# Column sums of the modulation by transposition and a VectorE reduction; head and norm spreads by transposition

## The chip, the core and the metric

The kernel runs on one core of a Trainium2 chip. The metric is the device time of one execution in microseconds (us), the median of several runs. The profile shows one execution; its times are counted from the start of its span.

## The reference, cut to what matters

Two layers work on x of 1024 tokens by 1024 features, all in f32: layer 0 mixes tokens by sliding-window attention, layer 1 by gated spatial mixing, and each is followed by a dense MLP. Each of the four sub-layers starts with a norm that is modulated by a vector made from c:

```python
cond = jax.nn.silu(c)
for i in range(DEPTH):                                   # DEPTH = 2
    mod = (cond @ mod_w[i] + mod_b[i])[:, None, :]       # mod_w[i]: 1024 x 6144
    shift1, scale1, gate1, shift2, scale2, gate2 = jnp.split(mod, 6, axis=-1)
    h = rms_norm(x, norm1_gain[i]) * (1 + scale1) + shift1
    y = swa_sink_attention(...) if i == 0 else gmlp_spatial_gating(...)
    x = x + gate1 * y
    h = rms_norm(x, norm2_gain[i]) * (1 + scale2) + shift2
    x = x + gate2 * squared_relu_mlp(h, w1[i], w2[i])
```

`rms_norm` divides each token by the root of its mean square over the features. In the attention, the queries of each head (64 features) are normed in the same way, and rotated by their position.

## The kernel before, in words

Features lie on the 128 partitions, tokens along the free dimension; x is 8 tiles of 128 x 1024. Every large product is made of units: 128 output features by 1024 tokens, 8 steps over the input features, each step three products (high by high, high by low, low by high, in a reduced f32 type that TensorE streams in one pass) for each half of 512 tokens. These are the matmuls of L1095, 48 a unit, 194 units. Units alternate between the PSUM tensors `pp[0]` and `pp[1]`. ScalarE makes the high part of a weight block (`split_hi`, L305) when the unit that used the buffer two units ago is done, GpSimd the low part (`split_lo`, L274), TensorE waits for it in `ready`. The engines run separate programs, and only semaphores tie them. The order of work on TensorE is written out by hand: small work is put between the steps of a unit by hooks.

**Modulation.** Its 12 parts (shift, scale, gate, twice a layer) of 1024 values each are sums over the 1024 features of c. VectorE multiplies rows of `mod_w` by a value of silu(c) for each partition and adds them up in `mod_acc` (128 x 1024; L668, L815). What is left is the sum over partitions. `mod_columns` (L1160 to L1167) does it on TensorE: eight f32 products with 128 columns of `mod_acc` as the weights and one column of ones as the moving operand write eight columns of `pp[3]`. VectorE's `mod_part` (L678 to L685, or L822 for parts 0 and 1) adds the bias, writes `mod`, and clears `mod_acc`. Parts 0 and 1 are made ahead of the first product, from `mod_acc` and from `tmp`, into different columns of `pp[3]`; part 2 is made in the stage of the queries, part 3 ahead of the attention, 4 and 5 in its output projection (5 inside `closing_pair`), 6 to 9 in the first MLP, 10 and 11 in the gated mixing.

**Head norms.** For five units (four of queries, one of keys), TensorE sums squares (`token_sums`, L1172), ScalarE takes the root, VectorE the reciprocal, and ScalarE copies each value 32 wide into `tmp` (L391). TensorE's `spread` (L1179) turns that by eight f32 products of 128 x 128 with the identity, so that features lie on partitions again; VectorE then rotates (L864 to L879).

**Norms 1 to 3** run half by half over `closing_pair` and `opening_pair`: TensorE sums squares (`token_squares`, L1187), ScalarE takes the root (L320), VectorE's `deviations` (L687 to L694) takes the reciprocal and writes the four values of a half as four diagonal matrices of 128 x 128 into `mod_t` (L691), and TensorE's `spread_norm` (L1195) multiplies them by a matrix of ones, which puts each token's value on all partitions. VectorE waits for it (`bc_done`), then scales x (L748) and makes the low part of h (L756), ScalarE makes the high part between the two (L341); TensorE's opening steps wait for that (`h_done`). Norm 0 has the same steps on whole rows.

`pp[3]` also takes the transposed values (L1236, which ScalarE copies at L447) and half of the attention's scores (L1246), and `pp[2]` the transpositions of the gated mixing (`v_turn`, L1344).

Of the kernel before, what the change touches and what calls it, by code (L numbers as in the profile page):

```python
# [14 lines left out]
P = 128  # L15
KC = D // P
HALF = 512
# [31 lines left out]
def build(nc, x_in, c_in, pos_in, weights, mod_w, cols, mats, ws_in, bias_in, q_dram, v_dram, out):  # L49
    f32, f32r, i32 = mybir.dt.float32, mybir.dt.float32r, mybir.dt.int32  # L50
    ALU = mybir.AluOpType
# [3 lines left out]
    with ctx:  # L55
        def sb(name, shape, dt=f32, where=ctx):
            return where.enter_context(nc.sbuf_tensor(name, shape, dt))

        def sem(name):
            return ctx.enter_context(nc.semaphore(name))  # L60
# [13 lines left out]
        vscale = sb("vscale", [P, 2, KC])  # L74
        root = sb("root", [P, 4 * KC])
        inv = sb("inv", [P, 4 * KC])
        qgain = sb("qgain", [P, 2])


# [94 lines left out]
        ws_ld, wsz = sem("ws_ld"), sem("wsz")  # L174
        sp_mm, t_mul, t_hi = sem("sp_mm"), sem("t_mul"), sem("t_hi")
        late_in = [sem("late_in0"), sem("late_in1")]
        acc_zero = sem("acc_zero")
        saved = sem("saved")


# [16 lines left out]
        def columns_of(half):  # L197
            return slice(HALF * half, HALF * half + HALF)
# [451 lines left out]
        def _(dve):  # L650
# [27 lines left out]
            def mod_part(part):  # L678

                dve.wait_ge(mod_mm, part + 1)  # L680
                V.tensor_tensor(out=mod[:, bass.ds(part, 1), :].rearrange("p a k -> p (a k)"),
                                in0=pp[3][:, HALF:HALF + KC], in1=colt[:, bass.ds(part * KC + 4 * KC, KC)],
                                op=ALU.add).then_inc(mod_done, 1)
                V.memset(mod_acc[:, :], 0.0).then_inc(acc_zero, 1)
                dve.wait_ge(acc_zero, part)  # L685

            def deviations(n, half):  # L687

                dve.wait_ge(sd_done, 2 * n + half + 1)
                own(V.reciprocal(inv[:, 4 * half:4 * half + 4], root[:, 4 * half:4 * half + 4]))  # L690
                V.tensor_tensor(out=mod_t[:, 0, columns_of(half)].rearrange("p (b m) -> p b m", m=P),  # L691
                                in0=ident[:, :].unsqueeze(1).to_broadcast([P, 4, P]),
                                in1=inv[:, 4 * half:4 * half + 4].unsqueeze(2).to_broadcast([P, 4, P]),
                                op=ALU.mult).then_inc(rb_done, 1)  # L694

            def gains(n):
                dve.wait_ge(mod_done, 3 * n + 2)
# [121 lines left out]
                        deviations(0, half)  # L819
            for part in range(2):  # L820
                dve.wait_ge(mod_mm, part + 1)
                V.tensor_tensor(out=mod[:, part, :], in0=pp[3][:, HALF * (1 - part):HALF * (1 - part) + KC],  # L822
                                in1=mod_b(part), op=ALU.add).then_inc(mod_done, 1)
            norm(0)
            V.memset(mod_acc[:, :], 0.0).then_inc(acc_zero, 1)
            dve.wait_ge(acc_zero, 1)
# [254 lines left out]
        def _(pe):  # L1081
# [75 lines left out]
                            spread_norm(n, 1)  # L1157
                last.then_inc(gemm, 1)

            def mod_columns(part, counter, count, acc=None, place=HALF):  # L1160

                pe.wait_ge(counter, count)
                acc = mod_acc[:, :] if acc is None else acc
                for k in range(KC):
                    last = T.matmul(pp[3][:, place + k:place + k + 1], acc[:, P * k:P * k + P], ones[:, 0:1],
                                    start=True, stop=True)
                last.then_inc(mod_mm, 1)  # L1167

            def token_sums(heads, select, counter):
# [6 lines left out]
            def spread(counter):  # L1176

                for b in range(KC):
                    last = T.matmul(pp[2][:, P * b:P * b + P], tmp[:, 1, P * b:P * b + P], ident[:, :],  # L1179
                                    start=True, stop=True)  # L1180
                last.then_inc(counter, 1)

            def token_squares(n, half):
# [8 lines left out]
            def spread_norm(n, half):  # L1192

                pe.wait_ge(rb_done, 2 * n + half + 1)
                T.matmul(pp[2][:, columns_of(half)], ones[:, :], mod_t[:, 0, columns_of(half)],  # L1195
                         start=True, stop=True).then_inc(bc_done, 1)

            pe.wait_ge(const_in, 48)
            for half in range(2):
# [1 line left out]
            mod_columns(0, mf_used, KC)  # L1201
            for half in range(2):
                spread_norm(0, half)
            mod_columns(1, mf_used, 2 * KC, tmp[:, 0, :], 0)

            def head_squares(j):

# [23 lines left out]
            for j in range(4):  # L1231
                if j:
                    pe.wait_ge(v_cp, j)
                for r in range(4):
                    n = 4 * j + r
                    last = T.transpose(pp[3][:, P * r:P * r + P], vt[:, CHUNK * n:CHUNK * n + P], ident[:, :])  # L1236
                last.then_inc(v_tr, 1)
            mod_columns(3, mt_used, 2 * KC)


# [78 lines left out]
            def mlp(layer):  # L1319
                pair0 = U_MLP[layer] // 2  # L1320
                opening_pair(pair0, 2 * layer + 1)
                h_units(pair0, 1)

                def down(g, close=None):
                    columns = (lambda: mod_columns(g + 6, mt_used, g * KC + (RING_MLP + KC))) if layer == 0 else None
                    hid_units(g * 8 + (pair0 + 4), g * KC + HID_MLP[layer], columns, close)

                down(0)
                with pe.Fori(1, MLP_GROUPS - 1 + layer) as g:
                    h_units(g * 8 + pair0, 0)  # L1330
                    down(g)
                if layer == 0:
                    h_units((MLP_GROUPS - 1) * 8 + pair0, 0)
                    down(MLP_GROUPS - 1, 2)
# [127 lines left out]
```

## Time and profile before

| | |
|---|---|
| median of 3 runs | 2522.09 us (2521.42 to 2524.6) |
| profiled execution | 2525.77 us, of which span 2523.8 us |
| TensorE busy | 96% of the span, mean granted clock 0.979 of full speed |
| VectorE, ScalarE, GpSimd busy | 40%, 25%, 20% |
| DMA | 189 MB, 75 GB/s mean |

A row of the timeline shows the start, then the length from the first start to the last end of a run of equal instructions, the engine, the line, the names out<-in, the shape and how many, and in brackets how long the engine had been idle and what ended that. The length of a matmul holds its way through the array; what a matmul costs in a stream is the distance from its start to the next one's. An f32 product appears as two records.

### The profile page before, as it was taken

The numbers are of one execution on the slowest core, as the hardware profiler recorded it, in microseconds if no ns is written. First come the engines' busy times: TensorE is split into PE (matmuls) and PEld (weight loads), VectorE is DVE, ScalarE is ACT, GpSimd is POOL, SyncE is SP. The second block draws the span as 40 slices with busy tenths as digits, with TensorE's granted clock in tenths as the row PEclk, the third lists the DMA queues.
The fourth block names the chain that finished last, engine by engine and source line by source line (L and its number), as shares of the span: only waits on it lengthen the run. The fifth ranks groups of instructions, "written<-read, shape, count | busy, mean of one in ns | idle before, by whom it ended". The sixth has DMA issues, their size and how long they took to land.

```text
span 2523.8 us, 28427 instructions
## 1 busy us (share of the span) xinstructions
PE 2418.9 (96%) x10592; PEld 1937.7 (77%) x10592; DVE 1011.1 (40%) x1088; ACT 633.1 (25%) x768; POOL 506.3 (20%) x232
## 2 busy tenths in 40 slices
PE   3997999999999999998999999999899999999999
PEld 2776677788888888886788888888688888888887
DVE  7664756532432333334432541343623322223232
ACT  3322622321221212222322221121321221222221
POOL 1111321121212212121211112112122212222121
PEclk9996999999999999998999999999899999999999
DMA  6342141221311211211333321221111111111112
GB/s 245 101 140 74 48 163 42 75 70 47 100 59 58 84 66 57 93 55 37 124 127 125 108 82 50 66 68 50 34 42 50 42 50 50 42 50 49 43 50 83
DMA packets 70594, 189.05 MB, mean 75 GB/s; under 512 B 23440, under 2 KB 25360, under 8 KB 70032
## 3 DMA queue, kind: packets, MB, share of 16 engines
q1 hardware_dynamic: 52144, 127.64, 15.8%
q10 hardware_dynamic: 18400, 60.69, 6.8%
q8 instruction: 37, 0.61, 0.1%
q14 instruction: 13, 0.11, 0.0%
HBM read 170.48 MB, written 16.78 MB: 74 GB/s over the span
## 4 chain that ended last, share of the span: by engine, by line
issue 64%; PE 28%; POOL 8%; POOLq 0%; DVE 0%; ACT 0%; DVEq 0%
PE pp L1095 28%; POOL w_lo L274 7%; POOL pr L286 1%; POOLq L294 0%; POOLq L273 0%; DVE x L969 0%; DVE mod_t L665 0%; ACT tmp L314 0%; POOLq L285 0%; POOLq L290 0%; POOLq L280 0%; POOL kf L277 0%; POOLq L274 0%; DVEq L969 0%; POOL vt L278 0%
## 5 line engine op out<-in xcount | busy, mean ns | idle before, releaser
L274 POOL TENSOR_TENSOR w_lo<-w_raw,w_hi 128x1024 fp32r<-128x1024 f32 x194 | 472.5, 2436 | 1922.9 <-ACT w_hi L305 1922.8
L1095 PE MATMUL pp<-h_hi,w_hi 128*128 128x512 f32 x1824 | 603.3, 406 | 35.2 <-DVE h_lo L756 23.3
L1095 PE MATMUL pp<-h_lo,w_hi 128*128 128x512 f32 x1824 | 592.8, 401 | 0.0
L1095 PE MATMUL pp<-h_hi,w_lo 128*128 128x512 f32 x1824 | 592.1, 400 | 0.0
L1095 PEld LDWEIGHTS pp<-h_hi,w_hi 128*128 128x128 f32 x1824 | 345.3, 192 | 127.8 <-issue 21.2
L305 ACT ACTIVATE w_hi<-w_raw 128x1024 fp32r<-128x1024 f32 x194 | 205.0, 1057 | 910.1 <-PE pp L1095 831.4
L1095 PEld LDWEIGHTS pp<-h_lo,w_hi 128*128 128x128 f32 x1824 | 348.9, 191 | 84.9 <-issue 1.0
L1095 PEld LDWEIGHTS pp<-h_hi,w_lo 128*128 128x128 f32 x1824 | 348.1, 191 | 85.1
L1095 PE MATMUL pp<-hid_hi,w_hi 128*128 128x512 f32 x1280 | 410.3, 398 | 0.0
L1095 PE MATMUL pp<-hid_lo,w_hi 128*128 128x512 f32 x1280 | 408.8, 396 | 0.0
L1095 PE MATMUL pp<-hid_hi,w_lo 128*128 128x512 f32 x1280 | 408.8, 396 | 0.0
L969 DVE SCALAR_TENSOR_TENSOR x<-pp,mod,x 128x1024 f32 (+1 forms) x82 | 104.8, 1278 | 493.8 <-PE pp L1095 493.7
L1095 PEld LDWEIGHTS pp<-hid_lo,w_hi 128*128 128x128 f32 x1280 | 241.1, 188 | 59.1 <-issue 0.5
L1095 PEld LDWEIGHTS pp<-hid_hi,w_lo 128*128 128x128 f32 x1280 | 241.1, 188 | 58.8
L1095 PEld LDWEIGHTS pp<-hid_hi,w_hi 128*128 128x128 f32 x1280 | 240.6, 188 | 58.5 <-issue 0.5
L993 DVE SCALAR_TENSOR_TENSOR tmp<-pp,tmp 128x1024 f32<-128x1024 f32 x64 | 78.4, 1224 | 335.9 <-ACT tmp L544 335.9
L665 DVE TENSOR_TENSOR mod_t<-mod_t,tmp 128x1024 f32<-128x1024 f32 x82 | 153.6, 1873 | 95.8 <-ACT tmp L314 95.0
L544 ACT ACTIVATE tmp<-pp 128x1024 f32<-128x1024 f32 x64 | 65.7, 1027 | 472.2 <-PE pp L1095 472.2
L996 DVE TENSOR_TENSOR hid_lo<-tmp,hid_hi 128x1024 f32 x64 | 119.3, 1864 | 87.0 <-ACT hid_hi L547 87.0
L668 DVE SCALAR_TENSOR_TENSOR mod_acc<-mod_t,cond,mod_acc 128x1024 f32<-128x1024 f32 x64 | 95.6, 1494 | 55.6 <-DMA mod_t<-mod_w 54.3
L314 ACT ACTIVATE tmp<-x 128x1024 f32 (+1 forms) x82 | 86.9, 1061 | 81.7 <-DVE x L969 73.6
L547 ACT ACTIVATE hid_hi<-tmp 128x1024 f32 x64 | 67.9, 1062 | 35.4 <-DVE tmp L993 35.4
(132 smaller groups left out, 1134.3 us busy)
## 6 DMA issues: line engine op xcount, KB each, us to landing
w_raw<-weights SPq DMA_DIRECT2D x194, 512.0 KB, 3.3
mod_t<-mod_w ACTq DMA_DIRECT2D x64, 512.0 KB, 3.4
mod_first<-mod_w SPq DMA_DIRECT2D x16, 512.0 KB, 15.5
mod_late<-mod_w ACTq DMA_DIRECT2D x2, 4096.0 KB, 19.1
v_dram<-v_out ACTq DMA_DIRECT2D x16, 512.0 KB, 5.3
vf<-v_dram ACTq DMA_DIRECT2D x16, 512.0 KB, 3.3
x<-x_in SPq DMA_DIRECT2D x4, 1024.0 KB, 9.0
qf<-q_dram SPq DMA_DIRECT2D x32, 128.0 KB, 2.5
```

What stands on the lines that cost most here:

```text
L274: nc.gpsimd.tensor_tensor(out=w_lo[:, s, :, :], in0=w_raw[:, s, :, :], in1=w_hi[:, s, :, :].bitcast(f32), op=ALU.subtract).then_inc(lo_don ...
L286: nc.gpsimd.tensor_tensor(out=pr[:, b, :, 0:P], in0=pr[:, b, :, 0:P], in1=small[:, b, 3, :].unsqueeze(2).to_broadcast([P, 4, P]), op=ALU.m ...
L305: nc.scalar.activation(w_hi[:, s, :, :], w_raw[:, s, :, :], ACT.Copy).then_inc(hi_done, 1)
L314: nc.scalar.activation(tmp[:, s, :], x[:, bass.ds(k, 1), :].rearrange("p a s -> p (a s)"), ACT.Square).then_inc(sq_done, 1)
L544: nc.scalar.activation(tmp[:, s, :], pp[s][:, :], ACT.Relu).then_inc(relu, 1)
L547: nc.scalar.activation(hid_hi[:, bass.ds(i * 2 + s, 1), :].rearrange("p a s -> p (a s)"), tmp[:, s, :], ACT.Copy).then_inc(hd_hi, 1)
L665: V.tensor_tensor(out=sumsq, in0=sumsq, in1=tmp[:, s, :], op=ALU.add).then_inc(ss_done, 1)
L668: V.scalar_tensor_tensor(out=mod_acc[:, :], in0=tile, scalar=cond[:, 2, bass.ds(k, 1)], in1=mod_acc[:, :], op0=ALU.mult, op1=ALU.add).then ...
L969: V.scalar_tensor_tensor(out=xn, in0=pp[s][:, :], scalar=mod[:, gate, bass.ds(i * 2 + s, 1)], in1=xn, op0=ALU.mult, op1=ALU.add).then_inc( ...
L993: V.scalar_tensor_tensor(out=tmp[:, s, :], in0=pp[s][:, :], scalar=0.0, in1=tmp[:, s, :], op0=ALU.max, op1=ALU.mult).then_inc(evac[s], 1)
L996: V.tensor_tensor(out=hid_lo[:, bass.ds(i * 2 + s, 1), :].rearrange("p a s -> p (a s)"), in0=tmp[:, s, :], in1=hid_hi[:, bass.ds(i * 2 + s ...
L1095: last = T.matmul(pp[s][:, cs], w[:, s, k, :], r[:, k, cs], start=(k == 0 and w is w_hi and r is hi), stop=(k == KC - 1 and w is w_lo))
```

## The change

`mod_columns` turns the eight blocks of `mod_acc` by transpositions into all 1024 columns of `pp[3]`, and VectorE sums each block of 128 columns by a reduction into `col_sum`, waits for it, and adds the bias. As all columns are written, TensorE waits for the part before (`mod_done`), and ahead of part 3 for the last copy of the values (`v_cp`). `spread` and `spread_norm` become transpositions with the identity; `deviations` writes each value 128 wide by a copy where it wrote diagonals.

```diff
             def mod_part(part):
                 dve.wait_ge(mod_mm, part + 1)
+                V.tensor_reduce(out=col_sum[:, :], in_=pp[3][:, :].rearrange("p (k c) -> p k c", c=P), axis=X,
+                                op=ALU.add).then_inc(col_summed, 1)
+                dve.wait_ge(col_summed, part + 1)
                 V.tensor_tensor(out=mod[:, bass.ds(part, 1), :].rearrange("p a k -> p (a k)"),
-                                in0=pp[3][:, HALF:HALF + KC], in1=colt[:, bass.ds(part * KC + 4 * KC, KC)],
+                                in0=col_sum[:, :], in1=colt[:, bass.ds(part * KC + 4 * KC, KC)],
                                 op=ALU.add).then_inc(mod_done, 1)
...
-                V.tensor_tensor(out=mod_t[:, 0, columns_of(half)].rearrange("p (b m) -> p b m", m=P),
-                                in0=ident[:, :].unsqueeze(1).to_broadcast([P, 4, P]),
-                                in1=inv[:, 4 * half:4 * half + 4].unsqueeze(2).to_broadcast([P, 4, P]),
-                                op=ALU.mult).then_inc(rb_done, 1)
+                V.tensor_copy(mod_t[:, 0, columns_of(half)].rearrange("p (b m) -> p b m", m=P),
+                              inv[:, 4 * half:4 * half + 4].unsqueeze(2).to_broadcast([P, 4, P])).then_inc(rb_done, 1)
...
             for part in range(2):
                 dve.wait_ge(mod_mm, part + 1)
-                V.tensor_tensor(out=mod[:, part, :], in0=pp[3][:, HALF * (1 - part):HALF * (1 - part) + KC],
-                                in1=mod_b(part), op=ALU.add).then_inc(mod_done, 1)
+                V.tensor_reduce(out=col_sum[:, :], in_=pp[3][:, :].rearrange("p (k c) -> p k c", c=P), axis=X,
+                                op=ALU.add).then_inc(col_summed, 1)
+                dve.wait_ge(col_summed, part + 1)
+                V.tensor_tensor(out=mod[:, part, :], in0=col_sum[:, :], in1=mod_b(part), op=ALU.add).then_inc(mod_done, 1)
...
-            def mod_columns(part, counter, count, acc=None, place=HALF):
+            def mod_columns(part, counter, count, acc=None):
                 pe.wait_ge(counter, count)
+                if part is not None:
+                    pe.wait_ge(mod_done, part)
                 acc = mod_acc[:, :] if acc is None else acc
                 for k in range(KC):
-                    last = T.matmul(pp[3][:, place + k:place + k + 1], acc[:, P * k:P * k + P], ones[:, 0:1],
-                                    start=True, stop=True)
+                    last = T.transpose(pp[3][:, P * k:P * k + P], acc[:, P * k:P * k + P], ident[:, :])
                 last.then_inc(mod_mm, 1)
...
             def spread(counter):
                 for b in range(KC):
-                    last = T.matmul(pp[2][:, P * b:P * b + P], tmp[:, 1, P * b:P * b + P], ident[:, :],
-                                    start=True, stop=True)
+                    last = T.transpose(pp[2][:, P * b:P * b + P], tmp[:, 1, P * b:P * b + P], ident[:, :])
...
             def spread_norm(n, half):
                 pe.wait_ge(rb_done, 2 * n + half + 1)
-                T.matmul(pp[2][:, columns_of(half)], ones[:, :], mod_t[:, 0, columns_of(half)],
-                         start=True, stop=True).then_inc(bc_done, 1)
+                for b in range(4 * half, 4 * half + 4):
+                    last = T.transpose(pp[2][:, P * b:P * b + P], mod_t[:, 0, P * b:P * b + P], ident[:, :])
+                last.then_inc(bc_done, 1)
...
-            mod_columns(1, mf_used, 2 * KC, tmp[:, 0, :], 0)
+            mod_columns(1, mf_used, 2 * KC, tmp[:, 0, :])
...
+            pe.wait_ge(v_cp, 4)
             mod_columns(3, mt_used, 2 * KC)
```

The calls for parts 6 to 9 pass `None`, and so don't wait for `mod_done`.

## Rows read from the trace of the kernel before

**Rows 1.** The page: busy time by engine.
```profile
PE 2418.9 (96%) x10592; PEld 1937.7 (77%) x10592; DVE 1011.1 (40%) x1088; ACT 633.1 (25%) x768; POOL 506.3 (20%) x232
```
**Rows 2.** Who waited for whom on TensorE from 230 us on (us, times, longest).
```profile
PE pp L1095 <- DVE h_lo L756: 23.3, 12, 4.0
```
**Rows 3.** Timeline of TensorE around the columns of part 6.
```profile
549.07 1.84 PE L1165 MATMUL pp<-ones,mod_acc 128*128 128x1 f32 x16
550.77 0.71 PE L1095 MATMUL pp<-hid_hi,w_hi 128*128 128x512 f32 x2
```
**Rows 4.** Timeline of TensorE around a `v_turn` (a transposition of eight blocks).
```profile
1228.02 1.03 PE L1344 MATMUL pp<-ident,tmp 128*128 128x128 f32 x8
1228.81 0.71 PE L1095 MATMUL pp<-h_hi,w_hi 128*128 128x512 f32 x2
```
**Rows 5.** Timeline of the query stage, TensorE, then VectorE.
```profile
133.13 1.95 PE L1179 MATMUL pp<-ident,tmp 128*128 128x128 f32 x16
134.83 0.71 PE L1095 MATMUL pp<-h_hi,w_hi 128*128 128x512 f32 x2
...
157.57 1.84 PE L1172 MATMUL pp<-colt,tmp 128*128 128x4 f32 x16
...
135.11 1.22 DVE L864 TENSOR_TENSOR tmp<-cos,pp 128x1024 f32<-128x1024 f32 x1 [7.35 <-PE pp L1179]
...
154.90 1.22 DVE L859 TENSOR_TENSOR tmp<-tmp 128x1024 f32<-128x1024 f32 x1
```
**Rows 6.** Lines of VectorE, shapes apart (count, then busy us, mean ns).
```profile
L911 DVE TENSOR_REDUCE small<-pp 128x4 f32<-128x516 f32 x30 | 20.5, 685 | 1.3 <-PE pp L1246 1.3
```
**Rows 7.** VectorE operations with one SBUF source (L1041: duration ns min, median, max).
```profile
74.80 0.69 DVE L830 TENSOR_SCALAR cos<-sin 128x1024 f32<-128x1024 f32 x1
...
L1041 DVE TENSOR_SCALAR vf<-vf,vscale x128: 330/336/2501, 1405.5 to 1682.4; 128x128 f32<-128x128 f32 x128
```
**Rows 8.** Timeline ahead of the attention.
```profile
227.68 3.41 PE L1165 MATMUL pp<-ones,mod_acc 128*128 128x1 f32 x16
234.18 3.78 PE L1246 MATMUL pp<-kf,qf 64*128 64x128 f32 x16 [3.09 <-DMA kf<-oa]
```
**Rows 9.** Timeline of the gated mixing after part 11.
```profile
1399.32 0.17 DVE L681 TENSOR_TENSOR mod<-pp,colt 128x8 f32<-128x8 f32 x1 [4.10 <-PE pp L1165]
...
1407.03 0.61 ACTq L617 DMA_DIRECT2D bias<-bias_in  x1
...
1410.29 2.02 PE L1370 MATMUL pp<-ws,vf 128*128 128x128 f32 x16 [1.05 <-issue]
```
**Rows 10.** Timeline of the closing and opening of norm 1.
```profile
423.91 1.02 PE L1195 MATMUL pp<-mod_t,ones 128*128 128x512 f32 x2
...
425.00 0.39 PE L1095 MATMUL pp<-h_lo,w_hi 128*128 128x512 f32 x1
...
424.73 1.05 ACT L305 ACTIVATE w_hi<-w_raw 128x1024 fp32r<-128x1024 f32 x1
...
442.28 0.69 DVE L691 TENSOR_TENSOR mod_t<-ident,inv 128x512 f32<-128x512 f32 x1
...
449.87 1.41 DVE L748 SCALAR_TENSOR_TENSOR tmp<-x,amp,pp 128x512 f32<-128x512 f32 x2 [2.46 <-PE pp L1195]
```
**Rows 11.** Timeline of the start: GpSimd, VectorE, TensorE.
```profile
29.16 6.06 POOL L274 TENSOR_TENSOR w_lo<-w_raw,w_hi 128x1024 fp32r<-128x1024 f32 x2 [28.13 <-ACT w_hi L305]
...
33.14 2.63 DVE L691 TENSOR_TENSOR mod_t<-ident,inv 128x512 f32<-128x512 f32 x1
...
47.30 0.16 DVE L822 TENSOR_TENSOR mod<-pp,colt 128x8 f32<-128x8 f32 x1
51.05 0.17 DVE L822 TENSOR_TENSOR mod<-pp,colt 128x8 f32<-128x8 f32 x1 [3.59 <-PE pp L1165]
```
**Rows 12.** Stretches: us, busy of PE, PEld, DVE, ACT, POOL, then the granted clock.
```profile
90.00:100.00 10.00, 8.35 (x28) 7.28 (x29) 2.78 (x3) 6.25 (x7) 0.00 (x0) 0.51 0.29 95
...
1200.00:1400.00 200.00, 198.50 (x928) 160.69 (x928) 68.70 (x161) 54.94 (x56) 39.25 (x16) 1.00 0.40 131
```

More of the change, by code:

```diff
@@ L76, in build @@
         inv = sb("inv", [P, 4 * KC])
+        col_sum = sb("col_sum", [P, KC])
         qgain = sb("qgain", [P, 2])
@@ L176, in build @@
         late_in = [sem("late_in0"), sem("late_in1")]
-        acc_zero = sem("acc_zero")
+        acc_zero, col_summed = sem("acc_zero"), sem("col_summed")
         saved = sem("saved")
@@ L1324, in down @@
                 def down(g, close=None):
-                    columns = (lambda: mod_columns(g + 6, mt_used, g * KC + (RING_MLP + KC))) if layer == 0 else None
+                    columns = (lambda: mod_columns(None, mt_used, g * KC + (RING_MLP + KC))) if layer == 0 else None
                     hid_units(g * 8 + (pair0 + 4), g * KC + HID_MLP[layer], columns, close)
```

## The prediction

> **What bounds the kernel now.** I read the busy times first: TensorE is busy for 96% of the span, the others for 40% or less [rows 1]. So in most places a microsecond taken from TensorE's stream is a microsecond of the kernel, and work on VectorE is free if it fits between its waits. The waits of TensorE then show where this is not so: from the attention on, most of what it waits for is VectorE's low part of h (L756), 23.3 us in 12 waits, four in each of the three openings [rows 2]. There the chain of VectorE and ScalarE sets the time. The timeline gives three more such places: the query stage, where the rotation on VectorE and the next head norm follow each other in a ring; the start, where parts 0 and 1 must be there before the first product; and the join in the gated mixing after part 11. I cost the change at each place by what is late there.
>
> **A transposition against a product.** The columns of part 6 take 549.07 to 550.77, 1.70 us for 16 records [rows 3]. `spread` takes the same 1.70 (133.13 to 134.83) [rows 5]. A `v_turn`, which is the very call that the change uses, with eight blocks and the identity, takes 1228.02 to 1228.81, 0.79 us for 8 records, and is followed by the same first product of a unit [rows 4]. So each of both saves 1.70 - 0.79 = 0.91 us of TensorE at the full clock. `spread_norm` takes 423.91 to 425.00, 1.09 us with one product in between that costs 0.24 at the pace of its neighbours, so 0.85 [rows 10]; four transpositions are half of a `v_turn`, about 0.40 with what the first product after them loses. It saves 0.45; for VectorE's start I count 0.43.
>
> **The reduction.** It reads 1024 f32 of PSUM in one pass. The reduction of 516 takes 0.685 [rows 6], a multiply over 1024 of PSUM 1.22 [rows 5]; I take 1.22, and 0.04 for its semaphore, an estimate from gaps of VectorE's dependent pairs: 1.26 us a part. Between ends of 1.2 and 1.4 nothing changes sign. The Trainium skill, "VectorE: DVE Perf Modes", section "Rules for kernel authors", speaks against it: a reduction on the hot path is to be expected at one element a cycle, the slowest kind of VectorE work. The row agrees on the rate; whether it is on the hot path is the question of each place.
>
> **The copy in `deviations`.** The product with the identity takes 0.69 for 512 elements [rows 10]. An operation with one SBUF source does 1024 in 0.69 [rows 7], so 512 cost about 0.43: 0.26 saved. The source repeats one value 128 times, which no row shows for VectorE; the bounds are a saving of 0 and of 0.26, and I take 0.26, as the row is the nearest in kind. The Trainium skill (same page, "Mode 2×_2P") has that rate for copies in SBUF when the outermost dimension is even, which it is here (4); with its figures the result is the same.
>
> **Parts 4 to 10** lie in TensorE's stream with no idle time ahead of the next step. VectorE's 1.26 us more is covered: VectorE's evacuation after part 6 is needed only when the next unit on the other buffer is done, and a unit takes over 10 us (at most 12.5, 2418.9 us on 194 units [rows 1]). After part 4, VectorE is behind by about 1.3 us at one evacuation, but the buffer is wanted some 10 us later. The new wait for `mod_done` looks back one part and is met long before. 7 x 0.91 = 6.4 us saved. Without the cover each would cost 1.26 - 0.91 = 0.35 instead.
>
> **Part 11** is different: its L681 at 1399.32 is followed on VectorE by `mod_acc`'s clearing, the aggregates of the layer norm and a memset, which release ScalarE's last load at 1407.03, and TensorE stands idle 1.05 us until the first blend at 1410.29 [rows 9]. The chain starts 0.91 earlier and is 1.26 longer: 0.35 us lost.
>
> **The query stage: five spreads and part 2.** VectorE waits 7.35 us for the spread, then begins the rotation that leads to the next head norm [rows 5]. Both TensorE's stream and that ring start 0.91 earlier, whichever is late. Five times 0.91 is 4.55. Part 2 takes 0.91 out of the stream ahead of the next sums at 157.57. These need VectorE's sum of squares, 154.90 + 1.22 = 156.1: 1.4 us of slack. The reduction uses 0.35 of it and the earlier stream 0.91, which leaves 0.1 or more. 0.91 saved, with 0.9 at risk. Stage: 5.5 us.
>
> **Part 3** has a clock of one half: 16 records in 3.41, so eight transpositions take about 1.8 and 0.25 to the end. It now waits for ScalarE's last copy of the values, of 512 columns, for which I take 0.9 us (VectorE needs 0.69 for 516 [rows 6], and the call has to be released). 227.7 + 0.9 + 2.05 + 1.26 gives 231.9, and the bias, the clearing and the sinks, 1.6 us at most, end near 233.5. The scores wait for a DMA until 234.18 anyway [rows 8]. Cost nothing; 0.6 us of cover, queued behind it is only the clearing of a buffer. If it fails, some tenths.
>
> **The three closings and openings.** In the first half, `spread_norm` is earlier for VectorE, but ScalarE splits the next weights until 425.78 and the high part follows only then; then GpSimd's pass holds VectorE [rows 10]. That chain starts from the unit before, so I count nothing (between 0 and 0.43 each). In the second half VectorE is waited for: its copy at 442.28 releases TensorE's restart, 0.26, and it then waits 2.46 us for the second `spread_norm` until 449.87, 0.43. 3 x 0.69 = 2.1 us saved.
>
> **The start.** VectorE's first diagonals at 33.14 take 2.63 since GpSimd's pass runs until 35.22 [rows 11]; an operation with one source is held in the same way, up to 2.5 where the median is 0.34 [rows 7]. So the copies save 0.26 and 0.26, together 0.5, not 2. Against it stands a new chain: parts 0 and 1 now share the columns of `pp[3]`. TensorE must wait for part 0's reduction, and VectorE comes to that only after the sums of part 1, at 47.30 [rows 11]. Before, these ended, then the products (3.6), then 51.05. Now: 46.8 + 1.26 + 0.2 to `mod_done`, 8 transpositions at half clock 2.05, reduction 1.26: the bias is added at about 51.6. 0.6 us lost. If the copy is not held by GpSimd, the start gains 1.4 instead.
>
> **The sum.** -6.4 + 0.35 - 5.5 - 2.1 + 0.6 = -13.0 us. The profiled execution goes from 2525.77 to 2512.8, its span from 2523.8 to 2510.8; the median of the runs was 3.7 below it, so 2522.1 - 13.0 = 2509.1 us.
>
> **The rivals.**
> (a) More is gained: the first copy is not held, part 11 hides, and the first `spread_norm` counts. 2.0 + 1.26 + 1.3: 2504.5. Against it are the held rows and 1.05 us of idle time at the join. 0.10.
> (b) The reduction is on the path at every part, as at 11. Parts 2 and 4 to 10 then cost 0.35 each instead of saving 0.91: 8 x 1.26 = 10.1, and 2519.2, within 0.2%. Against it: VectorE is busy 40% [rows 1] and idle ahead of most evacuations. 0.08.
> (c) The transposition of these operands takes two records a block as the product did. No TensorE time is saved and the reductions remain: +1.3 at part 2 or 11, about +2 at the start: 2525. Against it: `v_turn` has one record a block [rows 4]. 0.02.
> (d) Slower: transpositions leave TensorE at its lower clock for a while. In the stretch from 90 to 100 us, after a stall, the granted clock is 0.51, the 1.2 GHz level, and half the time is lost [rows 12]. 13 bursts of transpositions are new in the full-speed stream outside the openings (parts 2 and 4 to 11, four spreads or more). If each cost a third of what that stretch lost, 1.6 us, it would be 21, and 2509.1 + 21 = 2530; it decides from 1.0 us each (13.0 / 13). Against it: the stretch from 1200 to 1400 has 16 `v_turn`s and a clock of 1.00 [rows 12]. 0.04. The Trainium skill, "TensorE: Matmul & The Clock Gate", section "Part 4: PE-mode transpose", says that the full clock does not engage for transpositions; the same rows speak against that for short bursts between products, and by it alone the time would be that of this rival.
> My forecast has the remaining 0.76.
>
> **How the numbers follow.** A measurement of this kernel can tell about 0.2%, 5 us, from no change. Faster by more than that are the forecast and (a): 0.86. Within it (b) and (c): 0.10. Slower: (d), 0.04. For the range I take (a) as the low end, 2504.5; upward the copy without its saving (1.3), part 2 lost (0.9), the evacuations after parts 4 and 5 late (1.8), and a restart in an opening whose clock rises later (1.5 in all): 2514.6. I widen that to 2515.5 for the scatter of medians (3 us between the runs of before).
>
> **What would show it.** Part 6 with 8 records in 0.79 us; spreads of 0.79; L911-like reductions of 1.22 on VectorE; deviations' copy of 0.43, the first one held until 35.2; part 1's transpositions starting about 48.3 and the first product at 56.2 instead of 55.67; the first blend of the gated mixing with more idle ahead of it, about 2.3 us; the granted clock unchanged. I am wrong if the copy is slow, if the ring of the query stage turns out to be timed by a DMA that does not start earlier, or if idle time appears behind the columns of parts 4 to 10.

## The result and the profile after

The changed kernel takes 2504.82 us, the median of four runs (2504.02 to 2508.65), against 2523.35 (2521.42 to 2524.68) for four runs of the kernel before beside them. The ratio is 0.993, 95% interval 0.9918 to 0.9941. The profiled execution went from 2525.77 us to 2504.02, its span from 2523.8 to 2502.1. The forecast was 2509.1 and faster; the time lies inside the range, near its low end. About 18 us were gained where 13.0 had been summed.

The lines of after stand in the order of the groups that they answer to. The page, busy time by engine (answers to [rows 1]):
```profile
PE 2386.4 (95%) x10472; PEld 1911.2 (76%) x10472; DVE 1028.7 (41%) x1100; ACT 632.5 (25%) x768; POOL 505.8 (20%) x232
```
The waits of TensorE from 230 us on (answers to [rows 2]):
```profile
PE pp L1099 <- DVE h_lo L758: 23.5, 16, 4.0
```
The timeline of TensorE, in order of time: the start [rows 11], the query stage [rows 5], ahead of the attention [rows 8], the opening of norm 1 [rows 10], the columns of part 6 [rows 3], the blend [rows 9]:
```profile
48.30 1.94 PE L1171 MATMUL pp<-ident,tmp 128*128 128x128 f32 x8 [10.81 <-DVE mod L827]
...
56.16 1.19 PE L1099 MATMUL pp<-h_hi,w_hi 128*128 128x512 f32 x2 [5.92 <-DVE h_lo L717]
...
154.82 2.62 PE L1177 MATMUL pp<-colt,tmp 128*128 128x4 f32 x16 [2.29 <-DVE tmp L863]
...
164.04 1.03 PE L1184 MATMUL pp<-ident,tmp 128*128 128x128 f32 x8
164.83 0.48 PE L1099 MATMUL pp<-h_hi,w_hi 128*128 128x512 f32 x1
...
230.24 3.78 PE L1252 MATMUL pp<-kf,qf 64*128 64x128 f32 x16 [3.64 <-DMA kf<-oa]
...
434.41 0.79 PE L1099 MATMUL pp<-h_hi,w_hi 128*128 128x512 f32 x1 [1.69 <-DVE h_lo L758]
...
539.02 1.04 PE L1171 MATMUL pp<-ident,mod_acc 128*128 128x128 f32 x8
539.81 0.72 PE L1099 MATMUL pp<-hid_hi,w_hi 128*128 128x512 f32 x2
...
1392.70 2.02 PE L1376 MATMUL pp<-ws,vf 128*128 128x128 f32 x16 [2.53 <-issue]
```
VectorE's new operations: the reductions of parts 2 to 11 by shape (count, then busy us, mean ns, then the idle time before them), and the copies of the norm roots (duration ns min/median/max) with what they replace in [rows 10, 11]:
```profile
L682 DVE TENSOR_REDUCE col_sum<-pp 128x8 f32<-128x1024 f32 x10 | 12.2, 1221 | 33.0 <-PE pp L1171 33.0
...
L695 DVE COPY mod_t<-inv x8: 426/427/2373, 33.1 to 1776.0; 128x512 f32<-128x512 f32 x8
```
And one stretch of the gated mixing (columns as in [rows 12]):
```profile
1199.01:1392.70 193.69, 191.17 (x894) 155.96 (x895) 70.20 (x174) 49.99 (x51) 38.51 (x17) 1.00 0.40 133
```
Before, the same restart of norm 1's opening:
```profile
443.69 0.79 PE L1095 MATMUL pp<-h_hi,w_hi 128*128 128x512 f32 x1 [1.96 <-DVE h_lo L756]
```
The prices hold. Part 6 takes 8 records and 0.79 us (539.02 to 539.81), a spread 0.79 (164.04 to 164.83), a reduction 1.22, a copy 0.43 and, next to GpSimd's pass at the start, 2.37. The start is late by 0.49 (56.16 for 55.67), the restart of an opening waits 1.69 instead of 1.96, part 3 is hidden by the DMA, the blend waits 2.53. Two things are not in the forecast. TensorE waits 2.29 us for VectorE's sum at 154.82, where before it did not wait at all. And the long stages without any wait are shorter by more than the transpositions in them can explain. For the second, take two passes of GpSimd that stand at the same places of the program, one early in MLP 0 and one at its end. Before:
```profile
472.23 2.40 POOL L274 TENSOR_TENSOR w_lo<-w_raw,w_hi 128x1024 fp32r<-128x1024 f32 x1 [2.04 <-ACT w_hi L305]
...
1172.60 2.41 POOL L274 TENSOR_TENSOR w_lo<-w_raw,w_hi 128x1024 fp32r<-128x1024 f32 x1 [16.58 <-ACT w_hi L305]
```
After:
```profile
462.50 2.40 POOL L275 TENSOR_TENSOR w_lo<-w_raw,w_hi 128x1024 fp32r<-128x1024 f32 x1 [2.04 <-ACT w_hi L306]
...
1156.45 2.41 POOL L275 TENSOR_TENSOR w_lo<-w_raw,w_hi 128x1024 fp32r<-128x1024 f32 x1 [16.50 <-ACT w_hi L306]
```
700.37 us became 693.95, 6.42 less. Four parts lie in between (6 to 9): 4 x 0.91 = 3.64. That leaves 2.78. The last MLP has no columns at all, so the change touches nothing there; from a like pass at its start (1822.72 and 1803.79) to the end of the span it went from 701.1 to 698.3, again 2.8 less. The stages' differences, from the rows above and the like ones:

| stage, us | before | after | difference |
|---|---|---|---|
| to the first product | 55.67 | 56.16 | +0.49 |
| to the first scores | 178.51 | 174.08 | -4.43 |
| to the pass early in MLP 0 | 238.05 | 232.26 | -5.79 |
| to the pass at its end | 700.37 | 693.95 | -6.42 |
| to the pass at the start of MLP 1 | 650.12 | 647.34 | -2.78 |
| to the end | 701.1 | 698.3 | -2.8 |

The sum is -21.7, the difference of the two spans. Single executions of one and the same kernel differ by several us in the second stage (below), so the medians of many runs, not this column, carry the verdicts.

### The profile page after: what moved, and what is told of

Read it like the earlier page. It is cut to its first block, busy times and chain, and to the rows that moved or that the text cites. A ratio compares the mean times of both kernels' runs of the same rounds, so it can differ in the third digit from the quotient of the medians.

```text
span 2502.1 us, 28207 instructions
## 1 busy us (share of the span) xinstructions
PE 2386.4 (95%) x10472; PEld 1911.2 (76%) x10472; DVE 1028.7 (41%) x1100; ACT 632.5 (25%) x768; POOL 505.8 (20%) x232
## 4 chain that ended last, share of the span: by engine, by line
issue 64%; PE 28%; POOL 8%; POOLq 0%; DVE 0%; ACT 0%; DVEq 0%
PE pp L1099 28%; POOL w_lo L275 7%; POOL pr L287 1%; POOLq L295 0%; POOLq L274 0%; DVE x L973 0%; DVE mod_t L666 0%; ACT tmp L315 0%; POOLq L286 0%; POOLq L291 0%; POOLq L281 0%; POOL kf L278 0%; DVEq L973 0%; POOLq L275 0%; POOL vt L279 0%
```

## The experiments

All were timed in five rounds beside the kernel before, whose medians were 2523.64 us (e1 to e4), 2522.12 (e5 to e8) and 2522.96 (e9 to e12). The question of the first four: is the surplus real, and does it come with the code or with the place of the buffers? The change declares `col_sum` in the middle of SBUF and so moves every buffer declared behind it by 32 bytes.

**e1, the kernel before, unchanged.**

> The kernel before, unchanged. Question: in the profiles, six products in a row took 1.406 us before and 1.400 us after, 0.4% over some 2000 us of products, about 8 us of the 21.7 us between the two spans, in stages that the change does not touch. Theory A (the pace belongs to the execution, not to the kernel): no difference to the kernel before in the timed rounds (within 2 us), and the pace in this profile may come out at either value. Theory B (the pace belongs to the code or its layout in memory): pace 1.406 here again, and 1.400 in the kernel after on the same chip.

Measured: 2523.04 (2520.11 to 2526.13, 11 runs), ratio 1.0001 (0.9992 to 1.001). The same kernel timed twice gives the same time. The stage between the two passes is 700.37 again, to the hundredth, while the second stage is 175.83 for 178.51: the long streams repeat, the query stage scatters.

**e2, the changed kernel, unchanged.**

> The kernel after, unchanged. Theory A: 13 to 14.5 us below the kernel before once both are timed in turn on one chip (the sum of the steps is 13.0), pace as in the run before it on this chip. Theory B: 21 to 22 us below, pace 1.400 us for six products while the unchanged kernel before has 1.406. In between (17 to 18, as the medians so far): part of the pace is the kernel's, or steps of the sum are too small by 4 us.

Measured: 2507.63 (2503.73 to 2508.27, 5 runs), ratio 0.9936 (0.9923 to 0.995). The gain is 12.6 to 19.4 us by the interval, the idle time at the sum 2.28 us, MLP 0 693.94. The surplus and the new wait are properties of the kernel, not of one execution.

**e3, before with an unused buffer.**
```
@@ sbuf, ahead of qgain
+        col_sum = sb("col_sum", [P, KC])
```

> The kernel before with one edit: the unused buffer col_sum of 8 columns is placed ahead of qgain, as in the kernel after, so that all later buffers lie 32 bytes further on each partition. Theory A: no difference (within 2 us). Theory B in its form 'layout': pace 1.400 and about 8 us faster.

Measured: 2517.91 (2513.37 to 2518.95, 7 runs), ratio 0.9974 (0.9962 to 0.9985). Not one instruction differs from before, and the kernel is 5.7 us faster. The two passes of e3:
```profile
472.04 2.39 POOL L275 TENSOR_TENSOR w_lo<-w_raw,w_hi 128x1024 fp32r<-128x1024 f32 x1 [2.04 <-ACT w_hi L306]
...
1169.65 2.40 POOL L275 TENSOR_TENSOR w_lo<-w_raw,w_hi 128x1024 fp32r<-128x1024 f32 x1 [16.53 <-ACT w_hi L306]
```
697.61, which is 2.76 below before and 3.66 above after. So the stage splits cleanly: 2.76 by the shift, 3.66 by the change, for which 3.64 was forecast. In unbroken chains of products the starts of e3 are 1.4000 us apart for six products, in before 1.4057, in every part of the trace and for `h` and `hid` alike: 0.4%.

**e4, the columns alone** (with `col_sum` in its place): all of `mod_columns` and `mod_part` changed, `spread` and `spread_norm` as before.
```
 in mod_columns
-  T.matmul(pp[3][:, place + k:place + k + 1], acc[...], ones[:, 0:1], ...)
+  T.transpose(pp[3][:, P * k:P * k + P], acc[:, P * k:P * k + P], ident[:, :])
```

> The column sums as changed (transpositions, reductions, waits); the spreads, the norm's product and its diagonals as before. By my sum: parts 4 to 10 save 6.4, part 2 saves 0.9, part 11 costs 0.35, and the start costs 1.1 (its copies are not faster), together 5.9 us faster. From the trace of the kernel after, part 2 saved nothing: then 5.0. A rival in which the reduction is on the path at every part: 3 us slower. If the excess over the sum sits in this part of the change: 9 to 10 us faster.

Measured: 2516.1 (2513.02 to 2518.3, 11 runs), ratio 0.9972 (0.9963 to 0.9981), 1.8 us below e3 (0.5 by the two ratios) where the terms of the forecast for this part come to -5.9 (parts 4 to 10 -6.4, part 11 +0.35, part 2 -0.9, start +1.1). MLP 0 is 693.95, so parts 6 to 9 give all that was forecast. The wait at the sum is there, 2.28 us, and the blend waits 2.61. The piece of the query stage from part 2's transpositions to the next head squares takes 40.18 for 37.07 in e3, 3.1 more where 0.9 less was forecast. That is the size of the missing 4 us, though the times of e3 and e4 alone are too coarse to place it.

**e5, before with 64 bytes at the same place.** The large buffers behind the new one start at an odd multiple of 32 bytes before. With 32 bytes more they start at a multiple of 64, with 64 more again at an odd multiple of 32.
```
+        pad = sb("pad", [P, 2 * KC])
```

> The kernel before with an unused buffer of 16 columns (64 bytes a partition) in place of the 8 columns (32 bytes) that made six products in a row take 1.400 us instead of 1.406 and the kernel some 6 us faster. Theory 'alignment' (the large operands start at an odd multiple of 32 bytes before, and at a multiple of 64 after): a shift by 64 bytes changes nothing, pace 1.406, no difference within 2 us. Rival 'any shift, or more room between buffers, helps': pace 1.400, about 6 us faster.

Measured: 2517.46 (2514.8 to 2518.94, 10 runs), ratio 0.9979 (0.997 to 0.9988), MLP 0 697.53. As fast as with 32 bytes; alignment to 64 is not the cause.

**e6, the changed kernel with 32 bytes more.**
```
         col_sum = sb("col_sum", [P, KC])
+        pad = sb("pad", [P, KC])
```

> The kernel after with a further unused buffer of 8 columns, so that its large operands start at an odd multiple of 32 bytes as in the kernel before: the change without its shift. If the steps of my sum hold and the rest of the gain is the shift: pace 1.406 and 10 to 13 us below the kernel before. If the transpositions themselves gave more than the sum: 16 to 18 us below.

Measured: 2505.67 (2503.31 to 2508.55, 5 runs), ratio 0.9931 (0.9917 to 0.9944), MLP 0 693.93: no different from after. Its large buffers start at an odd multiple of 32 bytes again, as in before, and the pace stays the fast one; so this run did not take the shift away, and what the change gives without it is left to e9.

**e7, three repairs on top of the change**, for the places where the forecast or the trace has the reduction on the path. Part 1 gets PSUM of its own (`pp[1]`), so its transpositions need not wait for part 0's reduction. In the round of part 2, the third of four in the query stage, VectorE does the sum ahead of the accumulations. Part 11's reduction comes behind the first normalised block of the gated mixing.
```
 mod_columns(1, mf_used, 2 * KC, tmp[:, 0, :], pp[1])
 ...
 if j == 2:   # order on VectorE: part 2, the sum, two accumulations, reciprocal, one more
     mods(2)
     head_reciprocals(j, 4, lambda: mods(1))
 ...
 dve.wait_ge(mod_mm, 12)        # ahead of the memset of ws
 ...
 if kb == 0:                    # behind the first normalised block
     mod_part(11)
```

> The kernel after with three edits that take VectorE's reduction off the path: part 1 is transposed into pp[1], which is free then, so that TensorE doesn't wait for part 0 (start 1.4 us shorter); in the query stage VectorE adds the squares ahead of the next two steps of mod_acc, and takes the reciprocal ahead of the third (the 2.3 us of idle time and the slow clock behind it go: 2 to 4 us); part 11's reduction goes behind the first normalised block, so that the layer norm's aggregates start while TensorE still transposes (idle time ahead of the first blend 2.5 to 0: 2.5 us). Sum: 6 to 8 us below the kernel after, 22 to 25 below the kernel before. If these waits only move (to the DMA of the query stage, to the DMA of ws), 2 to 3 us below the kernel after.

Measured: 2497.41 (2496.64 to 2500.49, 4 runs), ratio 0.9902 (0.9887 to 0.9917): 8.3 us below e6, which ran beside it (7.3 by the two ratios), and 24.7 below the kernel before, as expected. Rows of its TensorE, then of its VectorE:
```profile
54.70 1.19 PE L1114 MATMUL pp<-h_hi,w_hi 128*128 128x512 f32 x2 [5.92 <-DVE h_lo L719]
...
152.38 1.84 PE L1192 MATMUL pp<-colt,tmp 128*128 128x4 f32 x16
...
148.23 1.62 DVE L685 TENSOR_TENSOR mod<-col_sum,colt 128x8 f32<-128x8 f32 x1
150.00 0.91 DVE L690 MEMSET mod_acc<- 128x1024 f32 x1 [0.16 <-issue]
150.95 1.23 DVE L870 TENSOR_TENSOR tmp<-tmp 128x1024 f32<-128x1024 f32 x1
```
The first product is at 54.70 for 56.16, 1.46 earlier. The sum starts at 150.95 for 153.55, ends before TensorE comes to it, and the wait is gone. The blend follows the stream without idle time. From the transpositions of part 2 to the next head squares it is 33.99 us for 39.22 in after. Not all of it reaches the end. Of the 1.46 nothing is left at part 2: its transpositions start at 145.84 in both, as the stretch from the second head squares to their spread took 9.21 us in e7 (122.13 to 131.34, granted clock 0.63) and 7.65 in after (123.70 to 131.35, 0.78). The first scores come 5.1 earlier, the stretch from the end of MLP 0 to the start of MLP 1 is 3.0 shorter, and the last MLP is 1.5 longer: TensorE waits 1.83 us at its start for GpSimd's low part, as in after (1.85), but the granted clock of the 5.4 us behind it is 0.68, and in after 1.00. 5.1 + 3.0 - 1.5 is 6.6, and the two spans differ by 6.7 (2502.1 and 2495.4).

**e8, the five spreads alone**, with the 32 bytes.
```
 in spread
-  T.matmul(pp[2][...], tmp[...], ident[:, :], start=True, stop=True)
+  T.transpose(pp[2][...], tmp[...], ident[:, :])
```

> The kernel before with the 32-byte shift and the head spreads by transposition alone. Against the shifted kernel (5.7 us below the kernel before) the sum says 5 x 0.91 = 4.6 us, so 10.3 below the kernel before. If the ring of the query stage were timed by a DMA that doesn't start earlier: 5.7 to 7.

Measured: 2513.32 (2512.26 to 2518.34, 9 runs), ratio 0.997 (0.996 to 0.998). That is 4.6 below e3, the very 5 x 0.91 = 4.55 of the forecast; but e3 ran in other rounds, and by the two ratios it is 1.0 us, so the agreement is in part luck. The runs of e8 stand in two groups, near 2512.5 and near 2518, with one between, so 4.6 is no sharp number; the 0.79 us of each spread in its trace is.

**e9, the change without the shift**: after, with `col_sum` declared behind every other buffer, so that each has the address it had before.
```
-        col_sum = sb("col_sum", [P, KC])      # ahead of qgain
+        col_sum = sb("col_sum", [P, KC])      # behind mod_t, the last
```

> The kernel after with col_sum allocated behind all other buffers, so that every other buffer has exactly the address it has in the kernel before: the change without its shift. If the pace of the products goes with the placement: six products in 1.406 us as before, and 10 to 12.5 us below the kernel before (the gain so far, 16 to 18, less the 5 to 6 that a shift alone gave). If it goes with anything else in the code: pace 1.400 and 16 to 18 us.

Measured: 2513.31 (2513.29 to 2517.7, 5 runs), ratio 0.9965 (0.9952 to 0.9979), 9.65 us below before, by the ratio 8.8, and 5.3 to 12.1 by the interval; 10 to 12.5 was expected. Its two passes:
```profile
467.68 2.40 POOL L275 TENSOR_TENSOR w_lo<-w_raw,w_hi 128x1024 fp32r<-128x1024 f32 x1 [2.04 <-ACT w_hi L306]
...
1164.41 2.40 POOL L275 TENSOR_TENSOR w_lo<-w_raw,w_hi 128x1024 fp32r<-128x1024 f32 x1 [16.57 <-ACT w_hi L306]
```
696.73: 3.64 below before, 2.78 above after. With e3 this closes the square: the change is worth 3.64 with the old places and 3.66 with the new, the shift 2.76 without the change and 2.78 with it. Six products are 1.4057 again.

**e10, before with 32 bytes ahead of all buffers**: every address moves, no distance between two buffers does.
```
+        pad = sb("pad", [P, KC])              # ahead of x, the first
```

> The kernel before with 32 unused bytes a partition ahead of all buffers: all distances between buffers as before, every address 32 further. If the pace goes with the distance between the weight blocks and h: 1.406, within 2 us of the kernel before. If it goes with the place of h itself: 1.400, 5 us faster.

Measured: 2523.63 (2520.48 to 2526.02, 11 runs), ratio 1.0003 (0.9994 to 1.0012), MLP 0 700.36, six products 1.4057. So the pace does not go with where the buffers stand by themselves, but with how far those behind the new one stand from those ahead of it.

**e11, before with 128 bytes at `col_sum`'s place.**
```
+        pad = sb("pad", [P, 4 * KC])
```

> The kernel before with an unused buffer of 128 bytes a partition ahead of qgain: h starts at the same address modulo 128 as before. If that residue sets the pace (before 32, the faster ones 64 and 96): 1.406, within 2 us of the kernel before. If not: 1.400, 5 us faster.

Measured: 2518.41 (2513.15 to 2519.2, 11 runs), ratio 0.9979 (0.997 to 0.9988), MLP 0 697.58. Fast again, so the remainder of the distance by 128 doesn't decide either. Of four distances (0, +32, +64, +128) only the old one is slow.

**e12, the norm roots alone**, with the 32 bytes: the copy in `deviations` and the transpositions in `spread_norm`.
```
-  V.tensor_tensor(out=mod_t[...], in0=ident..., in1=inv..., op=ALU.mult)
+  V.tensor_copy(mod_t[...], inv[...].unsqueeze(2).to_broadcast([P, 4, P]))
 in spread_norm
-  T.matmul(pp[2][:, columns_of(half)], ones[:, :], mod_t[...])
+  for b in range(4 * half, 4 * half + 4):
+      last = T.transpose(pp[2][:, P * b:P * b + P], mod_t[:, 0, P * b:P * b + P], ident[:, :])
```

> The kernel before with the 32-byte shift and only the norm's part of the change (copy in place of diagonals, spread by transposition). Against the shifted kernel: 3 x 0.69 + 0.5 at the start = 2.6 us, so about 8 us below the kernel before; seen in the trace: idle time ahead of the restart in each opening 1.69 in place of 1.95, and the stretch from there to the wait for GpSimd 0.4 shorter. If the gain of the first half counted too: 9.5. If the copy with its repeated source were no faster and the start didn't gain: 7.

Measured: 2514.48 (2510.78 to 2518.29, 7 runs), ratio 0.9969 (0.9957 to 0.9981), 3.4 below e3, by the ratios 1.3, where 2.6 was forecast. The restart waits 1.69 in all three openings. The time can't tell 2.6 from 1.3 or 3.4, and the trace gives nothing finer: the stretch from that restart to TensorE's next wait takes 12.7, 13.5 and 14.1 us in e12's own three openings, for the same work.

## The prediction, step by step

**The prices of single operations** were right: a transposition of eight blocks 0.79, reduction 1.22, copy 0.43, and 2.37 where GpSimd's pass holds it. This confirms the choice between the bounds for the copy: a source that repeats one value 128 times runs at the rate of the nearest row.

**Parts 4 to 10** were forecast at 0.91 each. Between the two passes four of them gave 3.64 and 3.66 in the two pairs that differ by the change alone. No idle time appeared behind them, although the bias adds of parts 6 to 9 took 1.42 to 1.61 us and not 0.17 (see part 2), which the same cover hid. **Parts 11 and 3** were right: 2.53 us of idle time for a forecast of about 2.3, and a DMA wait that grew from 3.09 [rows 8] to 3.64, the cover of part 3. **The start** came out at 56.16 for 56.2, its pieces at 48.30 for 48.3; e7 shows by its 1.46 us that the shared PSUM columns were the reason: with columns of its own, part 1 is turned while VectorE reduces part 0. **The openings**: the 0.26 is in every one of them; the 0.43 of the second half was neither shown nor refuted.

**The step that failed is part 2.** The forecast was 0.91 saved, "0.1 or more" of slack, "0.9 at risk". It became a wait of 2.29. VectorE's rows of after:
```profile
146.97 1.23 DVE L682 TENSOR_REDUCE col_sum<-pp 128x8 f32<-128x1024 f32 x1 [1.19 <-PE pp L1171]
148.23 1.62 DVE L685 TENSOR_TENSOR mod<-col_sum,colt 128x8 f32<-128x8 f32 x1
150.01 0.91 DVE L688 MEMSET mod_acc<- 128x1024 f32 x1 [0.16 <-issue]
150.96 2.67 DVE L669 SCALAR_TENSOR_TENSOR mod_acc<-mod_t,cond,mod_acc 128x1024 f32<-128x1024 f32 x2
153.55 1.22 DVE L863 TENSOR_TENSOR tmp<-tmp 128x1024 f32<-128x1024 f32 x1
```
GpSimd in the same stretch:
```profile
147.41 2.41 POOL L275 TENSOR_TENSOR w_lo<-w_raw,w_hi 128x1024 fp32r<-128x1024 f32 x1 [9.07 <-ACT w_hi L306]
```
And VectorE before:
```profile
150.53 0.17 DVE L681 TENSOR_TENSOR mod<-pp,colt 128x8 f32<-128x8 f32 x1 [2.04 <-PE pp L1165]
150.85 0.91 DVE L684 MEMSET mod_acc<- 128x1024 f32 x1 [0.16 <-issue]
151.80 3.18 DVE L668 SCALAR_TENSOR_TENSOR mod_acc<-mod_t,cond,mod_acc 128x1024 f32<-128x1024 f32 x2
```
Count both engines from the start of part 2's columns, 148.54 before and 145.84 after. VectorE's sum ended at +7.58 before (156.12) and ends at +8.93 after (154.77). The difference of nearly 1.4 is made of -0.85 for the transpositions, +1.27 for the reduction, +1.45 for the bias add, which takes 1.62 instead of 0.17, and -0.5 for the accumulations, which now run behind GpSimd's pass and not beside it. The bias add was not in the forecast at all. It has eight elements, but it read one operand from PSUM and now reads both from SBUF, and it ends when GpSimd's pass does, at 149.8. Before, the add at 150.53 also lay beside that pass (150.11 to 152.51) and took 0.17, with one source in SBUF; in after the same two-source add at 1381.67, with no pass beside it, takes 0.17 too. The other adds bear this out. In after, the five that lie beside a pass (parts 2 and 6 to 9) took 1.42 to 1.62 us, each to the end of the pass, and the seven others 0.17; in before, six lie beside a pass, and each took 0.17 or less. The Trainium skill, "GPSIMD Engine Reference", section "1. Specifications", says that GpSimd's interface to SBUF is shared with VectorE and that it contends with instructions that have two SBUF inputs; the 1.62 beside 0.17 agrees, and by that rule the step could have been foreseen.

TensorE, on its side, was ready at +9.03 before and is at +6.69 after: 2.34 earlier, 0.85 of it the transpositions. The other 1.5 is nearly all the clock, as the stretches show. Before, in the order columns of part 2, sums and products to the spread, then to the next head squares:
```profile
148.54:157.57 9.03, 9.03 (x40) 7.56 (x41) 5.29 (x5) 3.86 (x4) 2.40 (x1) 0.81 0.98 243
157.57:163.57 6.00, 6.00 (x35) 5.18 (x34) 1.55 (x2) 1.35 (x2) 0.00 (x0) 1.00 0.59 224
163.57:185.56 21.99, 20.22 (x95) 16.29 (x93) 16.87 (x12) 5.84 (x6) 5.72 (x2) 1.00 0.39 113
```
After:
```profile
145.84:154.82 8.98, 6.69 (x32) 5.26 (x33) 7.46 (x6) 3.86 (x4) 2.41 (x1) 1.00 1.00 242
154.82:164.04 9.22, 9.22 (x35) 7.75 (x36) 1.55 (x2) 1.34 (x2) 0.00 (x0) 0.63 0.42 157
164.04:185.06 21.02, 19.24 (x87) 15.28 (x86) 16.85 (x12) 5.83 (x6) 5.70 (x2) 1.00 0.40 115
```
And e7:
```profile
145.84:152.38 6.54, 6.54 (x33) 5.41 (x34) 5.18 (x5) 3.87 (x4) 2.41 (x1) 1.00 1.03 236
152.38:158.37 5.99, 5.99 (x35) 5.12 (x35) 2.54 (x3) 1.35 (x2) 0.00 (x0) 1.00 0.96 322
158.37:179.83 21.46, 19.25 (x87) 15.28 (x86) 17.80 (x13) 5.84 (x6) 4.79 (x2) 1.00 0.41 119
```
Before, the granted clock of the first stretch was 0.81. The slack of 1.4 us that I read in [rows 5] was time in which TensorE ran slowly; in after the clock was 1.00 there and the slack did not exist: 1.4 of slack, less 1.4 by which the sum is later, less 2.3 by which TensorE is earlier, is -2.3, the wait. e10 shows it without the change: same instructions as before, but a clock of 1.00 in this stretch.
```profile
152.18 1.22 DVE L860 TENSOR_TENSOR tmp<-tmp 128x1024 f32<-128x1024 f32 x1
...
145.81:153.45 7.64, 7.64 (x40) 6.22 (x40) 5.30 (x5) 3.87 (x4) 2.41 (x1) 1.00 0.99 230
```
TensorE comes to the sums at +7.64 there for +9.03, right behind the end of VectorE's sum (153.40), and no slack is left. The clock of this stretch is 0.81 in seven of the eight traces without the new columns, e10 being the eighth, and 1.00 in all six with them; why is not shown.

Behind the wait the clock falls to 0.63 in after, a mean between its two levels of 1.2 and 2.4 GHz, and the next stretch takes 9.22 for 6.00. The whole piece is 39.22 for 37.02 before, where the forecast had 37.02 - 2 x 0.91 = 35.2, so part 2 cost about 4 us more than planned here. In e9 the piece is 37.83 and in e6 37.87, some 2.6 more than planned. e7, with the order changed and nothing else in this piece, is at 33.99, below the forecast, as the clock stays at 1.00 throughout. That the wait comes from VectorE's order is shown by e7; why the clock behind the same wait (2.27 to 2.30 us) was 0.63 in after, e2 and e4 and 0.78 in e6 and e9 is not.

**The sum.** The change alone, e9, gave 9.65 for 13.0, and 13.0 lies above its interval (5.3 to 12.1). In the other places of the buffers, e2 against e3 in the same rounds, the change gave 10.3 (9.6 by the two ratios). The 2.7 to 3.4 that are missing are of the size of what part 2 lacks in the traces, 2.6 in e9 and about 4 in after. The change as it was made gave 16.2 to 17.7 by the ratios of its three comparisons (0.9936, 0.9931, 0.993). The rest, some 6 to 8 us, is the shift of the buffers, which without the change gave 5.7, 4.7 and 4.6 (e3, e5, e11; by the ratios 6.6, 5.3 and 5.3). The forecast had no term for it, though the change declares the buffer that does it. So 2509.1 was near 2504.82 in part by luck, because two errors of opposite sign stood in the sum: a missing loss of about 3 and a missing gain of 6 to 8. The sign and the largest term, parts 4 to 10, were right for the reasons given. Each spread is 0.91 shorter as forecast, but how much of the 4.55 reaches the end of the query stage is lost in the scatter of that stage.

**The rivals.** (a), more is gained, gave nearly the measured number, 2504.5, but by other causes, none of which came: the copy was held at the start, part 11 did not hide, and nothing shows that the openings gave more. (b), the reduction on the path everywhere, is true at parts 2 and 11 and at the start, and refuted at 4 to 10. (c) falls by the eight records of each transposition. (d), a lower clock behind transpositions, falls: in the stretch from 1199.01 to 1392.70, which holds the transpositions of parts 10 and 11 and sixteen `v_turn`s, it is 1.00 (the 2.4 GHz level), and 539.81 follows 539.02 at full pace. The Trainium skill, "TensorE: Matmul & The Clock Gate", section "Part 4: PE-mode transpose", would have the full clock not engage for them; no burst of eight in the stream shows that here. What stood ahead of the falls of the clock described above was a wait of TensorE.

## What to carry to other kernels

A slack of a microsecond between two engines must be read together with the granted clock of the stretch it lies in, and each small instruction whose operand moves from PSUM to SBUF must be looked at for a GpSimd pass beside it. Where a new reduction is put in a chain, ask at each place what else VectorE could do first; reordering three places was worth 7 to 8 us here, nearly as much as the change alone. And before a gain of a few tenths of a per cent is put down to an edit, take the edit's new buffer alone: a kernel with the same instructions and one unused buffer was 5.7 us faster.

## What the runs showed of the hardware that was not expected

**The pace of TensorE's products depends on the distance between buffers.** Six products of a unit (128x512 each) take 1.4057 us in before, e9 and e10, and 1.4000 in e3, e5, e11 and after: 2.8 us in 700. Moving everything by 32 bytes changes nothing; moving the buffers behind `qgain` against those ahead of it by 32, 64 or 128 gives the fast pace. Which pair of buffers it is (the declared order puts some operands of the products on either side) and what makes the old distance slow was not separated and stays open.

**A tiny VectorE instruction can be held until GpSimd's pass ends**: eight elements a partition, two sources in SBUF, 1.42 to 1.62 us beside a pass and 0.17 without. With one of the sources in PSUM it took 0.17 beside a pass too.

**A wait of TensorE is followed by a lower clock in some executions and not in others**, with the same length of wait: 1.85 us and a clock of 1.00 behind it in after, 1.83 and 0.68 in e7. Behind waits of 2.02 and 2.04 us ahead of the second head squares the clock was 0.78 in after and 0.63 in e7. The query stage holds most such places: before and e10, with the same instructions and the same pace, took 178.51 and 173.42 us from the first product to the first scores, 5.1 of the 5.2 us between their spans (2523.8 and 2518.6). That is about the 5 to 6 us by which runs of one kernel differ; the runs without a profile show no more than their times, so it is not shown that this explains them all.
